# Convolution sums of three SSM groups in PSUM, and end-weighted x made from the turned x in PSUM

## The chip, the cores and the metric

The kernel runs on one core of a Trainium2 chip. The metric is the device time of one execution in microseconds; a comparison takes the median of several runs. The engines are TensorE (PE in the profile; PEld are its weight loads), VectorE (DVE), ScalarE (ACT), GpSimd (POOL) and the DMA queues, most of them issued by SyncE (SP). Everything is 4-byte floating point; matrix products of the projections run on pairs of rounded parts (`hi` and `lo`, type fp32r).

## The reference

One step of a decoder with two layers, for a prompt of 16 + 512 tokens and for 8 sequences of 4 new tokens (32 columns, "decode"). The first layer is sliding-window attention, the second a Mamba-2 mixer. The change touches the second layer. There, cut to what matters:

```
z, xbc, dt = split(u @ w_in)
conv    = sum over 4 taps of conv_w[tap] * xbc shifted by tap       # per channel
xs, B, C = split(silu(conv + conv_b))                                # the convolution's output
dt      = softplus(dt + dt_bias);  a = cumulative sum of dt * A in a chunk of 128
y_diag  = (C B^T * exp(a_i - a_j), causal) @ (xs * dt)
states  = B^T @ (xs * dt * exp(a_end - a))                           # the end-weighted x
state   = state * exp(a_end) + states
y       = y_diag + (C @ state) * exp(a) + d_skip * xs
out     = rmsnorm(y * silu(z)) @ w_out
```

The decode sequences do the same from given convolution rows and given states, which are returned renewed.

## The kernel before

Activations lie with channels on the 128 partitions and the 560 tokens in columns. Weights come in slabs of 1 MB: SyncE loads one, ScalarE rounds it (`w_hi_buf`, L702), GpSimd subtracts to get the low part (`w_lo_buf`, L621, four pieces of 128x512 a slab), and TensorE makes three products per depth step (L1211 to L1213). A projection is done in halves of about 272 to 280 columns into the two banks of `pp` in turn; TensorE starts a half when the half before last has been evacuated by VectorE (`p_evac`).

The mixer runs in four groups g = 0 to 3 ("first" to "fourth group"). A group has six tiles of convolution input: B and C (tiles 0, 1) and x (2 to 5). `conv_in` (L1886) evacuates a half from `pp` into `rb`; `conv_tap` (L1905) copies the decode sequences' old rows, saves the new ones in `cn`, makes the first tap as `tensor_scalar` (L1921) and the other three as `scalar_tensor_tensor` (L1923), each reading `rb` and the sum `cv` and writing `cv`. The four depend on each other; `link` makes each wait for the one before. Both buffers `cv0` and `cv1` lie in SBUF and are used in turn; `silu_conv` (L945) on ScalarE turns them into `bc` and `xc`.

In groups 1 to 3 VectorE's order is written out by hand (L2093 to L2127): taps of tiles 0 to 2 between the evacuations of the group's own x tiles and the norm of the previous group's y (`norm_y`, L2065, and `low_y`, L2073), taps of tiles 3 to 5 between the evacuations of the previous group's out projection (`add_out`, L1709).

Then the chunks follow, in units u = 0 to 5 of the order decode, 16 meta tokens, and four chunks of 128. TensorE's `part_a` (L1447) makes C B^T and turns B and x into `pS`, with tokens on the partitions; VectorE's `prepare` (L1970) makes from it `cbm`, `btok`, `xdt` = x times dt, and `xw` = `xdt` times the end weights `wend`. `mix` (L2005) multiplies the decay matrix `seg` by `cbm`. `seg` is loaded by DMA, then `a_j` is subtracted by GpSimd (L673), then clamped and exponentiated by ScalarE (L1057, L1059). TensorE's `part_b` (L1516) makes the y product from `xdt` and `seg` into `pT_` (L1530), the product with the state (L1540) and the new state from `btok` and `xw` (L1544) into `pO`. GpSimd decays the state (L634) and VectorE adds (L2026).

For the decode unit, `prepare` splits `xw` into the parts `x_parts`, from which TensorE makes the outer products (L1501) that renew the states (L2168). Its end weights times dt are made as `dtw` (32x8) each time.

PSUM tensors are `pp`, `pS`, `pT_` and `pO`, two banks of 512 columns each. `pT_` and `pO` are in use during the chunks and idle in the groups' convolution phases, up to the turning of `cn` (L1626) into `pT_`.

Of the kernel before, what the change touches and what calls it, by code (L numbers as in the profile page):

```python
# [24 lines left out]
ACT = mybir.ActivationFunctionType  # L25
# [35 lines left out]
LOW_FROM = 5  # L61
STACK = 3 * SAMPLE

C_ID, C_MASK, C_CAUS, C_SMASK, C_LAST, C_BTOK, C_BEND, C_SUM4, C_RESET, C_SATT = np.cumsum(
# [99 lines left out]
def build(nc, x_prompt, x_sample, cache_k, cache_v, state_conv, state_ssm, meta_tokens, norm_w,  # L164
# [53 lines left out]
    with ctx:  # L218
# [3 lines left out]
        def at(name, shape, dt=F32, offset=None):  # L222
            size = int(np.prod(shape[1:])) * 4
            size += -size % 32
            if offset is None:
                offset, top[0] = top[0], top[0] + size
            assert offset + size <= nc.sbuf_usable_end, (name, offset + size)
            where[name] = offset
            return nc.alloc_sbuf_tensor_at(name, shape, dt, offset=offset)
# [82 lines left out]
        ealast = at("ealast", [P, 5, 32])  # L312
        dtw = at("dtw", [SAMPLE, SSM_H])
        dec_s = at("dec_s", [P, 16, DEC_B])
# [23 lines left out]
        fS, fT, fO = flat(pS), flat(pT_), flat(pO)  # L338
        misc = pO[:, 1, :]

        def sem(name):
# [59 lines left out]
        def conv_tile(g, i):  # L401

            return [16 + g, 20 + g][i] if i < 2 else 4 * g + i - 2
# [30 lines left out]
        def part_of(g, part):  # L434

            edge = EARLY if g + 1 < GROUPS else COL[3]
            return slice(edge, T) if part else slice(N_META, edge)

        def scale_of(g):
# [242 lines left out]
        def _(act):  # L682
# [262 lines left out]
            def silu_conv(g, i):  # L945
                k = 6 * g + i
                if i == 2 and g:
# [3 lines left out]
                b = conv_bc(conv_tile(g, i))  # L951
                act.activation(dst[:, 0:PROMPT], cv[k % 2][:, 0:PROMPT], ACT.Silu, bias=b)
                act.activation(dst[:, PROMPT:T].rearrange("p (b s) -> p b s", b=DEC_B),
                               cv[k % 2][:, PROMPT + HALO:CONV_IN].rearrange("p (b s) -> p b s", s=SEG)[:, :, 0:DEC_S],
                               ACT.Silu, bias=b).then_inc(act_ready, 1)
# [207 lines left out]
        def _(pe):  # L1163
# [398 lines left out]
            for g in range(GROUPS):  # L1562
# [58 lines left out]
                if g:  # L1621
                    pe.wait_ge(d_done, 5 * g)
                else:
                    pe.wait_ge(pt_ready, UNITS * GROUPS)
# [53 lines left out]
        def _(dve):  # L1678
# [226 lines left out]
            def conv_tap(g, i, tap):  # L1905
                k = 6 * g + i
                r, w, ct = rb[i % 3], cv[k % 2], conv_tile(g, i)
                if tap == 0:
# [61 lines left out]
            def prepare(g, u):  # L1970
# [7 lines left out]
                mask = cst[0:32, C_SMASK:C_SMASK + 32] if c == 5 else cst[0:n, C_CAUS:C_CAUS + n]  # L1978
                if v == 0:
                    dve.wait_ge(dec_ready, 1)  # L1980
                if c == 5:

# [3 lines left out]
                                      ALU.subtract).then_inc(b_ready, 1)  # L1986
                    link(dve.tensor_tensor(dtw[:, :], tok2[0:n, 0, c, hs], wend[0:n, c, hs], ALU.mult))
                    link(dve.tensor_tensor(heads(xw[0:n, b, :], n), heads(pS[0:n, 1, :], n), per_head(dtw[:, :], n),
                                           ALU.mult))
                    dve.tensor_copy(x_parts[64:96, :], xw[0:n, b, :])  # L1990
# [6 lines left out]
                if c:  # L1997
                    dve.tensor_tensor(cbm[0:n, b, 0:n], pS[0:n, 0, 0:n], mask, ALU.mult)
                dve.tensor_copy(btok[0:n, b, :], pS[0:n, 0, P:2 * P])
                link(dve.tensor_tensor(heads(xdt[0:n, b, :], n), heads(pS[0:n, 1, :], n),  # L2000
                                       per_head(tok2[0:n, 0, c, hs], n), ALU.mult))
                dve.tensor_tensor(heads(xw[0:n, b, :], n), heads(xdt[0:n, b, :], n),
                                  per_head(wend[0:n, c, hs], n), ALU.mult).then_inc(xw_done, 1)
# [232 lines left out]
```

## Time and profile before

| | us |
|---|---|
| median of 3 runs | 1008.78 (1008.69 to 1009.45) |
| span of the profiled execution | 1008.4 |
| TensorE busy | 974.3 (97%) |
| VectorE busy | 580.3 (58%) |
| ScalarE busy | 469.5 (47%) |
| GpSimd busy | 363.7 (36%) |

The span is the profiled execution's own time from the first to the last instruction of the program; what lies around it isn't in the profile. TensorE's matmuls overlap, and their ends are modelled, so its busy share says how seldom it waits, not how near its peak it is. A timeline row has the start in us, the duration in us of all instructions merged in the row, engine, line, operation, what is written and read, shape and count; in brackets stands the engine's idle time before it and what ended it. "issue" as a releaser means that the engine waited for nothing that the profile can name. Rows by line have the shortest, the median and the longest duration in ns.

### The profile page before, as it was taken

What the parts mean: (1) busy time and instruction counts of PE and PEld (TensorE: products, weight loads), DVE (VectorE), ACT (ScalarE), POOL (GpSimd) and SP (SyncE); (2) the same over time, 40 slices, a digit from 0 to 9 for tenths busy, and PEclk for the clock granted to TensorE, in tenths of its full rate; (3) what the DMA queues carried; (4) which work ended last, traced back from release to release, by engine and by line L of the source; (5) the groups of instructions that cost most, each with busy time, mean ns of one, the idle gap of its engine ahead of it and who ended that gap; (6) DMA issues with size and microseconds to landing.
All of it is one profiled execution on the core that took longest, in us unless ns stands there. A gap on an engine that the chain in (4) does not pass through costs nothing.

```text
span 1008.4 us, 18539 instructions
## 1 busy us (share of the span) xinstructions
PE 974.3 (97%) x7372; PEld 896.8 (89%) x7372; DVE 580.3 (58%) x1433; ACT 469.5 (47%) x819; POOL 363.7 (36%) x275
## 2 busy tenths in 40 slices
PE   9999999999999999999998999999999999999988
PEld 8998999889998999879988789997899888997877
DVE  4225431444224421356687779957798577886872
ACT  6435713463235612467355455244552545526453
POOL 2331234134231143116442445425344253543600
PEclk9999999999999999999999999999999999999989
DMA  6522223322223222102425624256341662426203
GB/s 201 194 67 83 65 85 112 103 83 84 84 70 144 84 84 90 44 21 61 131 88 151 188 71 124 73 159 180 87 137 45 170 178 77 137 64 211 76 11 100
DMA packets 144117, 106.35 MB, mean 105 GB/s; under 512 B 10258, under 2 KB 135364, under 8 KB 143840
## 3 DMA queue, kind: packets, MB, share of 16 engines
q1 hardware_dynamic: 117208, 92.25, 29.5%
q10 hardware_dynamic: 26824, 12.93, 4.8%
q8 instruction: 58, 0.95, 0.4%
q14 instruction: 27, 0.22, 0.1%
HBM read 92.44 MB, written 16.79 MB: 108 GB/s over the span
## 4 chain that ended last, share of the span: by engine, by line
PE 83%; DVE 10%; issue 3%; ACT 1%; POOL 1%; DMA 0%; ACTq 0%; SPq 0%; DVEq 0%; POOLq 0%
PE pp L1211 20%; PE pp L1213 19%; PE pp L1212 19%; PE pS L1327 3%; PE pS L1551 2%; DVE cv L1923 2%; PE pT_ L1530 1%; PE pO L1540 1%; PE pO L1544 1%; PE pO L1373 1%; PE pO L1372 1%; PE pO L1491 1%; POOL w_lo_raw L621 1%; PE pS L1463 1%; DVE z L2065 1%
## 5 line engine op out<-in xcount | busy, mean ns | idle before, releaser
L621 POOL TENSOR_TENSOR w_lo_buf<-w_raw_buf,w_hi_buf 128x512 fp32r<-128x512 f32 x214 | 287.4, 1374 | 485.4 <-ACT w_hi_buf L702 247.6
L1211 PE MATMUL pp<-h_hi,w_hi_buf 128*128 128x280 f32 (+1 forms) x1248 | 378.1, 303 | 5.2 <-DVE rb L1897 2.8
L1213 PE MATMUL pp<-h_hi,w_lo_buf 128*128 128x280 f32 (+1 forms) x1248 | 362.9, 291 | 0.0
L1212 PE MATMUL pp<-h_lo,w_hi_buf 128*128 128x280 f32 (+1 forms) x1248 | 362.2, 290 | 0.0
L1211 PEld LDWEIGHTS pp<-h_hi,w_hi_buf 128*128 128x128 f32 x1248 | 235.2, 188 | 16.0 <-issue 8.0
L1212 PEld LDWEIGHTS pp<-h_lo,w_hi_buf 128*128 128x128 f32 x1248 | 235.2, 188 | 4.6 <-issue 4.1
L1213 PEld LDWEIGHTS pp<-h_hi,w_lo_buf 128*128 128x128 f32 x1248 | 235.2, 188 | 0.0
L702 ACT ACTIVATE w_hi_buf<-w_raw_buf 128x2048 fp32r<-128x2048 f32 (+1 forms) x55 | 104.0, 1892 | 23.4 <-DMA w_raw_buf<-in_w_ssm_in 16.4
L1709 DVE TENSOR_TENSOR x<-x,pp 128x272 f32<-128x272 f32 (+3 forms) x128 | 56.4, 440 | 79.5 <-PE pp L1213 78.7
L1211 PE MATMUL pp<-og_hi,w_hi_buf 128*128 128x280 f32 (+2 forms) x256 | 75.5, 295 | 1.7 <-DVE og_lo L1830 1.1
L1213 PE MATMUL pp<-og_hi,w_lo_buf 128*128 128x280 f32 (+2 forms) x256 | 74.5, 291 | 0.0
L1212 PE MATMUL pp<-og_lo,w_hi_buf 128*128 128x280 f32 (+2 forms) x256 | 74.4, 290 | 0.0
L1923 DVE SCALAR_TENSOR_TENSOR cv<-rb,par,cv 128x584 f32<-128x584 f32 x69 | 70.0, 1015 | 1.1
L1211 PE MATMUL pp<-y_hi,w_hi_buf 128*128 128x272 f32 (+2 forms) x224 | 66.7, 298 | 1.1 <-DVE x L1709 0.9
L1212 PE MATMUL pp<-y_lo,w_hi_buf 128*128 128x272 f32 (+2 forms) x224 | 64.5, 288 | 0.0
L1703 DVE TENSOR_TENSOR q<-pp,rs 128x280 f32<-128x280 f32 x32 | 14.4, 450 | 77.9 <-PE pp L1213 77.9
L1057 ACT ACTIVATE seg<-seg 128x1024 f32<-128x1024 f32 (+1 forms) x20 | 18.6, 932 | 83.1 <-issue 47.9
L1213 PE MATMUL pp<-y_hi,w_lo_buf 128*128 128x272 f32 x192 | 55.5, 289 | 0.0
L1211 PEld LDWEIGHTS pp<-og_hi,w_hi_buf 128*128 128x128 f32 x256 | 48.1, 188 | 2.7 <-issue 2.6
L1782 DVE TENSOR_TENSOR gate<-pp,rs 128x280 f32<-128x280 f32 x32 | 14.4, 450 | 62.8 <-PE pp L1213 62.8
L1212 PEld LDWEIGHTS pp<-og_lo,w_hi_buf 128*128 128x128 f32 x256 | 48.2, 188 | 0.2 <-issue 0.2
L1213 PEld LDWEIGHTS pp<-og_hi,w_lo_buf 128*128 128x128 f32 x256 | 48.1, 188 | 0.0
(338 smaller groups left out, 1724.1 us busy)
## 6 DMA issues: line engine op xcount, KB each, us to landing
w_raw_buf<-in_w_attn_in SPq DMA_DIRECT2D x16, 1024.0 KB, 5.2
w_raw_buf<-in_w_ssm_in SPq DMA_DIRECT2D x16, 1024.0 KB, 5.4
w_raw_buf<-in_w_attn_out SPq DMA_DIRECT2D x8, 1024.0 KB, 5.0
s_in<-in_state_ssm SPq DMA_DIRECT2D x32, 256.0 KB, 4.2
out<-s_in SPq DMA_DIRECT2D x32, 256.0 KB, 3.2
seg<-a_scratch ACTq DMA_DIRECT2D x16, 512.0 KB, 4.5
w_raw_buf<-in_w_ssm_out SPq DMA_DIRECT2D x8, 1024.0 KB, 5.6
w_raw_buf<-in_w_attn_in SPq DMA_DIRECT2D x8, 512.0 KB, 6.3
```

The lines of the kernel that those rows point to most:

```text
L621: ins = pool.tensor_tensor(low_buf(n)[:, piece], raw[n % RAW_SLOTS][:, piece], high_buf(n)[:, piece].bitcast(F32), ALU.subtract)
L702: act.activation(high_buf(n)[:, 0:m], raw[n % RAW_SLOTS][:, 0:m], ACT.Copy).then_inc(w_hi, 1)
L1057: act.activation(e, e, ACT.Relu, scale=-1.0).then_inc(clamped, 1)
L1211: pe.matmul(dst, hi[:, k, cols], a_hi[:, k, tk], start=(k == 0), stop=False)
L1212: pe.matmul(dst, hi[:, k, cols], a_lo[:, k, tk], start=False, stop=False)
L1213: mm = pe.matmul(dst, lo[:, k, cols], a_hi[:, k, tk], start=False, stop=(k == depth - 1))
L1327: mm = pe.matmul(fS[0:n, h * 256:h * 256 + nk], q[:, h, COL[c]:COL[c] + n], kq[:, k0:k0 + nk], start=True, stop=True)
L1551: mm = pe.matmul(pS[:, part, 0:tk.stop - tk.start], ones[:, :], xc[:, t, tk], start=(t == 0), stop=(t == HEADS - 1))
L1703: dve.tensor_tensor(dst[:, tk], bank(kind, s, tile, half), rs[:, tk], ALU.mult).then_inc(p_evac, 1)
L1709: dve.tensor_tensor(x[:, tile, tk], x[:, tile, tk], bank("out", s, tile, half), ALU.add).then_inc(p_evac, 1)
L1782: dve.tensor_tensor(gate[:, t, tk], bank("gate", s, t, half), rs[:, tk], ALU.mult).then_inc(p_evac, 1)
L1923: ins = dve.scalar_tensor_tensor(w[:, 0:CONV_OUT], r[:, tap:tap + CONV_OUT], conv_wc(tap, ct), w[:, 0:CONV_OUT], ALU.mult, ALU.add)
```

## The change

Four things are changed.

1. In groups 1 to 3 (k = 6g + i of 6 or more) the sums of the taps are kept in PSUM: `taps_of(k)` gives 587 columns at the end of `pT_` for even tiles and of `pO` for odd ones, in the place of `cv0` and `cv1`. All four taps write there, three read there, and ScalarE's activation reads there. Group 0 stays in SBUF.
2. TensorE's turning of `cn` into `pT_` waits in groups 1 to 3 for the activation of tile 4 too, which reads `pT_`.
3. `wend` is multiplied by `tok2` (dt) once for all groups, in three instructions ahead of group 0's decode unit; `dtw` is gone.
4. `xw` is made from the turned x in `pS` and the multiplied `wend`, no longer from `xdt`; nothing waits for `xdt` between.

```diff
@@ -60,6 +60,7 @@
+TAPS_AT = 1024 - CONV_IN
@@ -310,7 +311,6 @@
-        dtw = at("dtw", [SAMPLE, SSM_H])
@@ -337,6 +337,7 @@
+        cv_psum = [fT[:, TAPS_AT:1024], fO[:, TAPS_AT:1024]]
@@ -436,6 +437,10 @@
+        def taps_of(k):
+
+            return cv[k % 2] if k < 6 else cv_psum[k % 2]
+
@@ -949,9 +954,9 @@
-                act.activation(dst[:, 0:PROMPT], cv[k % 2][:, 0:PROMPT], ACT.Silu, bias=b)
+                act.activation(dst[:, 0:PROMPT], taps_of(k)[:, 0:PROMPT], ACT.Silu, bias=b)
...
@@ -1620,6 +1625,7 @@
                 if g:
                     pe.wait_ge(d_done, 5 * g)
+                    pe.wait_ge(act_ready, 6 * g + 5)
@@ -1904,7 +1910,7 @@
             def conv_tap(g, i, tap):
                 k = 6 * g + i
-                r, w, ct = rb[i % 3], cv[k % 2], conv_tile(g, i)
+                r, w, ct = rb[i % 3], taps_of(k), conv_tile(g, i)
@@ -1977,16 +1983,19 @@
                 if v == 0:
+
                     dve.wait_ge(dec_ready, 1)
+                    for m, c0, c1 in ((P, 1, 5), (16, 0, 1), (SAMPLE, 5, 6)):
+                        ins = dve.tensor_tensor(wend[0:m, c0:c1, :], wend[0:m, c0:c1, :], tok2[0:m, 0, c0:c1, :], ALU.mult)
+                    link(ins)
...
-                    link(dve.tensor_tensor(dtw[:, :], tok2[0:n, 0, c, hs], wend[0:n, c, hs], ALU.mult))
-                    link(dve.tensor_tensor(heads(xw[0:n, b, :], n), heads(pS[0:n, 1, :], n), per_head(dtw[:, :], n),
-                                           ALU.mult))
+                    link(dve.tensor_tensor(heads(xw[0:n, b, :], n), heads(pS[0:n, 1, :], n),
+                                           per_head(wend[0:n, c, hs], n), ALU.mult))
@@ -1997,9 +2006,9 @@
-                link(dve.tensor_tensor(heads(xdt[0:n, b, :], n), heads(pS[0:n, 1, :], n),
-                                       per_head(tok2[0:n, 0, c, hs], n), ALU.mult))
-                dve.tensor_tensor(heads(xw[0:n, b, :], n), heads(xdt[0:n, b, :], n),
+                dve.tensor_tensor(heads(xdt[0:n, b, :], n), heads(pS[0:n, 1, :], n),
+                                  per_head(tok2[0:n, 0, c, hs], n), ALU.mult)
+                dve.tensor_tensor(heads(xw[0:n, b, :], n), heads(pS[0:n, 1, :], n),
                                   per_head(wend[0:n, c, hs], n), ALU.mult).then_inc(xw_done, 1)
```

VectorE in group 1's convolution phase, before; `rb_115` is the input of tile 2, `cv_117` and `cv_116` the sums of tiles 1 and 2:

```order
643 L1923 SCALAR_TENSOR_TENSOR cv_117<-rb_114,par,cv_117 128x584 x2
644 L1897 TENSOR_TENSOR rb_114<-pp,rs 128x280
645 L1913 COPY rb_115<-pS 128x8x3
646 L1919 COPY cn<-rb_115 128x3
647 L1920 COPY cn<-rb_115 128x24
648 L1921 TENSOR_SCALAR cv_116<-rb_115,par 128x584
649 L1923 SCALAR_TENSOR_TENSOR cv_116<-rb_115,par,cv_116 128x584
```

And in the changed kernel:

```order
645 L1929 SCALAR_TENSOR_TENSOR pO<-rb_114,par,pO 128x584 x2
646 L1903 TENSOR_TENSOR rb_114<-pp,rs 128x280
647 L1919 COPY rb_115<-pS 128x8x3
648 L1925 COPY cn<-rb_115 128x3
649 L1926 COPY cn<-rb_115 128x24
650 L1927 TENSOR_SCALAR pT_<-rb_115,par 128x584
651 L1929 SCALAR_TENSOR_TENSOR pT_<-rb_115,par,pT_ 128x584
```

No instruction has another place; only where the sum lies is different.

VectorE ahead of group 0's decode unit, before (from the first z evacuation to the first part of x):

```order
537 L2152 TENSOR_TENSOR z<-pp,rs 128x272
538 L1983 CAST b_parts<-pS 32x128
539 L1984 CAST b_parts<-pS 32x128
540 L1985 TENSOR_TENSOR b_parts<-pS,b_parts 32x128
541 L1987 TENSOR_TENSOR dtw<-tok_146,wend 32x8
542 L1988 TENSOR_TENSOR xw<-pS,dtw 32x512
543 L1990 CAST x_parts<-xw 32x512
```

And in the changed kernel:

```order
537 L2161 TENSOR_TENSOR z<-pp,rs 128x272
538 L1989 TENSOR_TENSOR wend<-wend,tok_146 128x128
539 L1989 TENSOR_TENSOR wend<-wend,tok_146 16x32
540 L1989 TENSOR_TENSOR wend<-wend,tok_146 32x32
541 L1993 CAST b_parts<-pS 32x128
542 L1994 CAST b_parts<-pS 32x128
543 L1995 TENSOR_TENSOR b_parts<-pS,b_parts 32x128
544 L1997 TENSOR_TENSOR xw<-pS,wend 32x512
545 L1999 CAST x_parts<-xw 32x512
```

Three multiplies stand ahead of everything of this unit, once in the program, and `dtw` is missing here and in the other three groups.

## Rows read from the trace of the kernel before

**Rows 1.** The page: the span, and part 1 (busy time, share, instructions).
```profile
span 1008.4 us, 18539 instructions
...
PE 974.3 (97%) x7372; PEld 896.8 (89%) x7372; DVE 580.3 (58%) x1433; ACT 469.5 (47%) x819; POOL 363.7 (36%) x275
```

**Rows 2.** Waits of TensorE from 560 us: total us, times, longest us.
```profile
PE pT_ L1530 <- issue: 8.2, 12, 1.0
PE pS L1551 <- ACT xc L1124: 4.0, 1, 4.0
PE pp L1211 <- DVE rb L1901: 2.3, 3, 1.2
PE pS L1501 <- DVE xdt L1994: 1.5, 3, 0.5
...
PE pp L1211 <- DVE x L1709: 1.3, 3, 0.4
PE pp L1211 <- DVE rb L1897: 0.8, 2, 0.5
```

**Rows 3.** Timeline of VectorE, second group (start, us, line, out<-in, count).
```profile
705.53 1.40 DVE L2002 TENSOR_TENSOR xw<-xdt,wend 128x512 f32<-128x512 f32 x1
...
708.03 1.74 DVE L2012 TENSOR_TENSOR seg<-seg,cbm 128x1024 f32<-128x1024 f32 x1 [0.49 <-ACT seg L1059]
```

**Rows 4.** Timeline of GpSimd, the same stretch.
```profile
695.88 2.29 POOL L673 TENSOR_TENSOR seg<-seg,tok 128x1024 f32<-128x1024 f32 x1 [5.14 <-DMA seg<-a_scratch]
...
699.14 1.89 POOL L673 TENSOR_TENSOR seg<-seg,tok 128x1024 f32<-128x1024 f32 x1
705.34 1.04 POOL L634 TENSOR_TENSOR state<-state,ealast 128x512 f32<-128x512 f32 x1 [4.31 <-PE pO L1544]
706.34 2.35 POOL L673 TENSOR_TENSOR seg<-seg,tok 128x1024 f32<-128x1024 f32 x1
```

**Rows 5.** Timeline of ScalarE, the same stretch.
```profile
706.93 1.06 ACT L1059 ACTIVATE seg<-seg 128x1024 f32<-128x1024 f32 x1
```

**Rows 6.** VectorE by line: count, duration ns min/median/max, first and last start.
```profile
L2002 DVE TENSOR_TENSOR xw<-xdt,wend x20: 691/1247/1631, 561.1 to 961.0; 128x512 f32<-128x512 f32 x16, 16x512 f32<-16x512 f32 x4
...
L2000 DVE TENSOR_TENSOR xdt<-pS,tok x20: 668/681/682, 560.4 to 960.3; 128x512 f32<-128x512 f32 x16, 16x512 f32<-16x512 f32 x4
...
L2168 DVE SCALAR_TENSOR_TENSOR s_in<-s_in,dec_s,pS x128: 328/344/349, 542.7 to 930.0; 128x128 f32<-128x128 f32 x128
...
L1923 DVE SCALAR_TENSOR_TENSOR cv<-rb,par,cv x69: 817/827/1747, 496.9 to 903.3; 128x584 f32<-128x584 f32 x69
...
L1921 DVE TENSOR_SCALAR cv<-rb,par x23: 508/518/1564, 496.3 to 900.0; 128x584 f32<-128x584 f32 x23
...
L1987 DVE TENSOR_TENSOR dtw<-tok,wend x4: 269/282/960, 537.7 to 911.3; 32x8 f32<-32x8 f32 x4
```

**Rows 7.** Timeline of VectorE, convolution phases of the second and third groups.
```profile
620.94 2.60 DVE L1923 SCALAR_TENSOR_TENSOR cv<-rb,par,cv 128x584 f32<-128x584 f32 x2
...
624.71 1.56 DVE L1921 TENSOR_SCALAR cv<-rb,par 128x584 f32<-128x584 f32 x1
626.31 1.75 DVE L1923 SCALAR_TENSOR_TENSOR cv<-rb,par,cv 128x584 f32<-128x584 f32 x1
...
743.53 2.33 DVE L2065 SCALAR_TENSOR_TENSOR z<-z,par,rg 128x160 f32<-128x160 f32 x4
```

**Rows 8.** Timeline of GpSimd, second group's convolution phase.
```profile
621.15 6.28 POOL L621 TENSOR_TENSOR w_lo_buf<-w_raw_buf,w_hi_buf 128x512 fp32r<-128x512 f32 x4 [5.36 <-ACT w_hi_buf L702]
```

**Rows 9.** Groups by line and shape of VectorE: count, busy us, mean ns.
```profile
L2023 DVE COPY state<-pO 128x512 f32<-128x512 f32 x4 | 2.7, 684 | 0.0
```

**Rows 10.** Timeline of VectorE, end of the second group's out projection.
```profile
655.97 0.44 DVE L1709 TENSOR_TENSOR x<-x,pp 128x272 f32<-128x272 f32 x1 [0.22 <-PE pp L1213]
657.48 0.44 DVE L1709 TENSOR_TENSOR x<-x,pp 128x272 f32<-128x272 f32 x1 [1.07 <-PE pp L1213]
```

**Rows 11.** Timeline of ScalarE, activation of tile 4, second group.
```profile
650.47 0.74 ACT L952 ACTIVATE xc<-cv,par 128x528 f32<-128x528 f32 x1 [3.63 <-DVE cv L1923]
```

More of the change, by code:

```diff
@@ L951, in silu_conv @@
                 b = conv_bc(conv_tile(g, i))
-                act.activation(dst[:, 0:PROMPT], cv[k % 2][:, 0:PROMPT], ACT.Silu, bias=b)
+                act.activation(dst[:, 0:PROMPT], taps_of(k)[:, 0:PROMPT], ACT.Silu, bias=b)
                 act.activation(dst[:, PROMPT:T].rearrange("p (b s) -> p b s", b=DEC_B),
-                               cv[k % 2][:, PROMPT + HALO:CONV_IN].rearrange("p (b s) -> p b s", s=SEG)[:, :, 0:DEC_S],
+                               taps_of(k)[:, PROMPT + HALO:CONV_IN].rearrange("p (b s) -> p b s", s=SEG)[:, :, 0:DEC_S],
                                ACT.Silu, bias=b).then_inc(act_ready, 1)
```

## The prediction

> **What bounds the kernel now.** I read the page first: the span is 1008.4 us and TensorE is busy for 974.3 of it [rows 1]. So nothing that VectorE saves is worth anything unless TensorE waits for it. The profiled execution's span stands 0.4 us below the median of the runs (1008.78), which I take as what lies around the span; the sum is made against 1008.4 and 0.4 is added at the end.
>
> Next the waits of TensorE, from 560 us on, where the groups' chunks begin [rows 2]. The reader is to see four kinds. Twelve waits before the product with `seg` (L1530), 8.2 us, put down to "issue", since what was waited for is a semaphore chain and not a neighbour; five before a projection for the evacuation into `rb` (L1901 2.3 us in three, L1897 0.8 in two), in the convolution phases; three of 0.5 us before the decode products (L1501); and one of 4.0 us in the last group. That is the purse: about 13 us can be touched by this change at all, the 4.0 us only by moving as a whole.
>
> Then what stands behind each kind. For L1530 I read the same stretch on three engines [rows 3 to 5]. VectorE makes `xw` at 705.53 from two SBUF tensors and is busy 1.40 us with it. GpSimd decays the state from 705.34 to 706.38 and then subtracts in `seg` from 706.34 for 2.35 us. The same subtraction took 1.89 us at 699.14, when no such VectorE instruction lay beside it. The rows are those of two engines that exclude each other: `xw` stands still until the decay ends, then holds the subtraction up for 2.35 - 1.89 = 0.46 us; ScalarE's exponent is ready at 707.99, but the multiply in `seg` (708.03, 1.74 us) ends at 709.77, which is 1.08 us after the subtraction's end at 708.69. TensorE waits for that multiply. The minimum, median and maximum by line say who is open to this [rows 6]: `xw<-xdt,wend` 691/1247/1631 ns, the taps 817/827/1747 and 508/518/1564, but `xdt<-pS,tok`, the same size with one source in PSUM, 668/681/682 in all 20, and the state update with a PSUM source 328/344/349 in all 128.
>
> **The chunks: xw from the turned x in PSUM.** 20 instructions go, 20 of the form of `xdt<-pS,tok` come: 0.68 each, never stretched. VectorE saves up to 0.72 us in a stretched one, but it idles before the multiply anyway; only what GpSimd gains reaches TensorE. At the third unit's chunk, `xw` holds the subtraction of 695.88 up by 2.29 - 1.89 = 0.40; at the next one by 0.46. After that, ScalarE's 707.99 against GpSimd's 708.23 says what is late next: it leaves the full 0.46 standing, with 0.24 to spare. At the last chunk no subtraction follows, so nothing is gained. A group gains 0.86; in each of the four groups the pattern has two such subtractions, so 3.4 us, of which I take 3.3. Bounds: 0 if ScalarE's chain or the landing of `seg` takes over at once, 4 groups by 3 waits by the mean wait of 0.68, that is 8.2, if all of them vanish. The dependence between `xdt` and `xw` goes too; not counted.
>
> A rule speaks against this edit. The Trainium skill, VectorE: DVE Perf Modes, section on the TRN2 errata, gives a VectorE instruction out of PSUM 62 cycles more fixed cost than one out of SBUF, 0.065 us each at its clock. The row disagrees: with the PSUM source 681, with both in SBUF 691 at best [rows 6]. By the rule `xw` would still be shorter than its median, and the sum would lose at most some 0.3 us where it lies on the path.
>
> **The decode unit.** `dtw` goes: 0.28 in three groups [rows 6], directly on the path from the turned x to the decode products, where TensorE waits 0.5 each time [rows 2]. So 0.8 us. In the first group `dtw` took 0.96 (the maximum), and three multiplies of `wend` by `tok2` come, once, ahead of everything of that unit. All have two SBUF sources, and a slab's split runs beside them. Priced as `dtw`: 3 x 0.27 = 0.8 to 3 x 0.96 = 2.9, less 0.96: from -0.1 to +1.9. I take +0.4, near the low end, since short instructions in a row mostly pass in one gap between GpSimd's.
>
> **The convolution: 18 tiles in groups 1 to 3.** Each has one tap of L1921 and three of L1923. Second and third groups show it [rows 7, 8]: from 620.94, beside GpSimd's split from 621.15, two taps take 2.60 instead of 2 x 0.82, a first tap 1.56 instead of 0.52, another tap 1.75. Three stretches of about 1 us stand ahead of the evacuation for which TensorE waited its 1.2 us. With the sum in PSUM a tap has one SBUF tensor source, as the 128 state updates have. No row shows VectorE writing PSUM, so a tap is bounded: 0.77 (the 0.82, less 0.05) below; above, if reading and writing one PSUM bank took turns, twice the slope per element. That slope is (827 - 344) / (584 - 128) = 1.06 ns, so 827 + 584 x 1.06 = 1.45 us. I take 0.82, the row of the same operation. The first tap: 0.52 at best as now. L2023, a one-source copy of 512 elements out of PSUM, takes 0.684 [rows 9], so 584 elements take 0.684 + 72 x 1.06 ns = 0.76. I take 0.76, +0.24 on a clean one.
>
> The Trainium skill, VectorE: DVE Perf Modes, section "Why PSUM operands drop a tier", says that any PSUM operand keeps a one-source instruction on 4-byte data from going two elements per cycle. It names operands in general; the trace shows it for a source only. By it the sum is the one I make; if a PSUM destination alone kept the fast mode, it would be 0.7 us lower.
>
> What reaches TensorE: the waits behind stretched taps, 1.2 in the second group, 0.3 in the third, 0.5 and 0.2 in the fourth, 2.2 of the 3.1 us [rows 2], go whole: in each of the three phases stretched taps stand ahead of the evacuation waited for (the longest is 1.75 [rows 6]), and 0.9 us of stretch outweighs 0.5 of wait. The one of 1.0 us in the third group does not: ahead of it stand four `norm_y` instructions with two SBUF tensors (743.53, 2.33 us) [rows 7], unchanged. The first taps before them are clean today, so +0.24 falls on it, and about as much on each sister evacuation in the second and fourth groups, which come just in time: +0.7. Net -1.5. The waits for `x<-x,pp` (1.3 us) [rows 2] come from `low_y`, two SBUF sources, unchanged.
>
> In the out projection, where twelve more taps stand between evacuations, a tile takes TensorE 1.51 us (655.97 to 657.48) [rows 10], and an evacuation with a tap at most 0.44 + 0.82 = 1.26: TensorE is waited for, not VectorE, and that stays. A first tap with its three small copies comes to some 1.7, once in four tiles; the second bank covers it.
>
> **The new wait.** TensorE's turning of `cn` now waits for the activation of tile 4. In the second group that begins at 650.47 [rows 11] and ends about a microsecond later, while TensorE is still delivering out tiles at 657.48 [rows 10] and has one z projection after. Cost 0, with some 6 us to spare. Behind it would stand all z projections. ScalarE now reads its input from PSUM; its 0.74 us changes by hundredths, in idle time.
>
> **Sum.** 1008.4 - 3.3 - 0.8 + 0.4 - 1.5 = 1003.2, with 0.4 around it 1003.6 us, 0.5% faster.
>
> **Rivals.**
> 1. ScalarE takes over in the chunks. Its exponent stands only 0.24 before the new end of GpSimd's subtraction, and behind it lies a loop (evacuation, three adds, DMA issue, two activations) that GpSimd's gain doesn't shorten. If that loop, not GpSimd, sets the pace, the 3.3 go: 1008.4 - 0.8 + 0.4 - 1.5 + 0.4 = 1006.9. For it: the closeness. Against it: the multiply ended 1.08 after GpSimd, not after ScalarE.
> 2. The convolution's gain is given back: freed taps bring VectorE earlier to `norm_y` and `low_y`, which meet GpSimd's split instead. In the second group the `norm_y` of this kind is clean and could become the third group's, +1.0. Then the convolution's net is 0: 1008.4 - 3.3 - 0.8 + 0.4 + 0.4 = 1005.1.
> 3. Slower. Taps that read and write the same PSUM bank take 1.45 us. It decides from 1.51 - 0.44 = 1.07 us per tap: above that, a tap and an evacuation no longer fit into an out tile. Nine such taps in the out phase cost 1.45 - 1.07 = 0.38 each, 3.4; nine ahead of it 0.6 each, 5.6, less the 3.1 that stretching costs today: about 6 a group, 18 in all, against 3.7 saved elsewhere: 1008.4 - 3.7 + 18 + 0.4 = 1023. Nothing in the trace has that form; for it only that no row excludes it.
> 4. The change frees VectorE and GpSimd, and neither term reaches TensorE, which is at 97% [rows 1]: rivals 1 and 2 together, 1008.4 - 0.8 + 0.4 + 0.4 = 1008.4. For it: most of what VectorE saves is saved while it idles.
>
> **How the numbers follow.** A change under 0.2% (2 us) can't be told from none here. Forecast case 0.60; rival 1 0.14; rival 2 0.12; rival 3 0.05; rival 4 0.09. Under 1006.76: the forecast case, rival 2 and half of rival 1: 0.79. Within 0.2%: the other half and most of rival 4: 0.14. Slower: rival 3 and the tail of 4: 0.07. The range must leave out no more than 0.2. Downwards, more of the 8.2 us at L1530 may go than I counted: 1000.8. Upwards, up to rival 1: 1007.3.
>
> **What would show it.** `xw` at 0.68 in all 20; the 128x1024 subtractions of `seg` at 1.89 with none above 2.0 except behind the multiply; L1530's waits down from 8.2 to about 5. Taps of 584 elements in groups 1 to 3 with a maximum near their median, about 0.82; first taps at 0.76. The 1.2 us wait of the second group gone, the 1.0 of the third still there. Wrong would be: taps above 1.07; L1530's waits as they were, with ScalarE's exponent as the last to arrive; a new wait of TensorE at the turning of `cn`.

## The result and the profile after

The changed kernel takes 1000.07 us (median of 4, 997.68 to 1002.94) against 1008.79 us beside it: a ratio of 0.9914, 95% interval 0.9892 to 0.9935. In a second session it took 1001.11 us (1000.03 to 1002.61), ratio 0.9918 [0.9902, 0.9934]. So it is 8 to 9 us faster, where 5.2 had been forecast; 1000.07 lies 0.7 us below the forecast range. The changed kernel's single times lie some 5 us apart, by how long TensorE ran at half clock; its profiled execution is one of the longer ones (1002.94). Two lines of the page answer to [rows 1]:

```profile
span 1000.9 us, 18538 instructions
...
PE 973.2 (97%) x7372; PEld 898.3 (90%) x7372; DVE 555.2 (55%) x1432; ACT 468.5 (47%) x819; POOL 347.7 (35%) x275
```

VectorE's busy time fell by 25 us and GpSimd's by 16; TensorE's stayed. What moved are the waits. The view of TensorE's waits from 560 us on (total us, times, longest), to be held against [rows 2]:

```profile
PE pT_ L1535 <- issue: 4.6, 8, 1.1
PE pS L1556 <- ACT xc L1129: 4.1, 1, 4.1
PE pS L1465 <- DVE s_in L2177: 2.1, 4, 1.4
...
PE pS L1506 <- DVE xdt L2003: 0.5, 3, 0.2
PE pp L1216 <- DVE x L1715: 0.4, 1, 0.4
```

The five waits for the evacuation into `rb` are gone, 0.9 of the 1.3 us for `x` too, and the wait for the product with `seg` went from 8.2 to 4.6 us. The 2.1 us before L1465 hold one wait of 1.4 in the fourth group.

The view by line (count, ns min/median/max, first and last start) says that none of these is stretched any more, against [rows 6]: `xw`, the subtraction in `seg`, and in groups 1 to 3 the taps with their sum in PSUM. (The three new multiplies in the first group are; they come below.)

```profile
L2011 DVE TENSOR_TENSOR xw<-pS,wend x20: 669/681/682, 563.4 to 953.6; 128x512 f32<-128x512 f32 x16, 16x512 f32<-16x512 f32 x4
...
L678 POOL TENSOR_TENSOR seg<-seg,tok x20: 607/1898/1903, 531.0 to 947.3; 128x1024 f32<-128x1024 f32 x16, 32x256 f32<-32x256 f32 x4
...
L1929 DVE SCALAR_TENSOR_TENSOR pT_<-rb,par,pT_ x27: 821/825/832, 610.3 to 889.3; 128x584 f32<-128x584 f32 x27
...
L1927 DVE TENSOR_SCALAR pT_<-rb,par x9: 816/822/826, 609.1 to 885.1; 128x584 f32<-128x584 f32 x9
```

Where the time went is read best from the starts of TensorE's work. I took in each trace the first start of four kinds of instruction: the turning of the old convolution rows (a group's start), the first out projection, the turning of `cn`, the first decode product (L1501, L1506). The lengths between them, as difference to the kernel before, in us (before's own lengths from its one trace):

| phase | before | changed kernel | forecast |
|---|---|---|---|
| first group, to the turning of `cn` | 41.2 | -0.5 | 0 |
| first group, to the first decode product | 7.3 | +1.90 | +0.4 |
| second to fourth group, the same | 6.04, 6.04, 6.03 | -0.32, -0.32, -0.31 | -0.28 each |
| chunks, first to third group | 61.3, 61.3, 61.4 | -0.80, -1.15, -0.88 | -0.86 each |
| convolution up to the out projection, second to fourth group | 28.42, 28.62, 28.31 | -1.60, -1.80, -1.49 | -1.5 in all |
| out projection and first z half, the same | 28.44, 28.15, 28.45 | -0.76, -0.48, -0.77 | 0 |

The changed kernel's three convolution phases have one length, 26.82 us, and no wait stands in them. The first phase, which the change doesn't touch, is 0.2 to 0.7 us shorter than in before's profile in all runs that don't touch it; I leave it out of the account. Between two executions of the changed kernel the other lengths agree within 0.03 us, the chunks within 0.3 where the clock is the same.

The fourth group's chunks have to be read with the clock. The rows are stretches of the trace: length, busy us of PE, PEld, DVE, ACT and POOL with counts, then the granted clock. Before:

```profile
914.70:972.10 57.40, 50.06 (x374) 41.56 (x374) 43.98 (x90) 27.52 (x41) 21.93 (x15) 0.91 0.43 128
```

The changed kernel in its profiled execution, and in another one (run `e8_same_again`):

```profile
906.50:964.50 58.00, 51.14 (x374) 42.68 (x374) 39.67 (x90) 27.64 (x42) 20.56 (x15) 0.88 0.43 127
```

```profile
908.00:961.50 53.50, 47.75 (x374) 39.43 (x374) 39.34 (x89) 27.57 (x42) 21.57 (x15) 0.97 0.47 137
```

A mean of 0.91 is 10.3 us at the lower level of 1.2 GHz (0.09 x 57.4 x 2), 0.88 is 13.9 us, 0.97 is 3.2 us. Between the two executions of the same kernel, 10.7 us more of it cost 4.5, so 0.42 us each, an estimate from one pair. Before's 7.1 us more than in the last row are worth 3.0 of its 3.9 us: the chunks gained about 0.9 here too. So without the clock the change is worth some 9.7 us, by this estimate: -6.9 in the convolution, -3.7 in the chunks, -0.95 in three decode units, +1.9 in the first.

### The profile page after: what moved, and what is told of

The parts are those of the page before. It is cut to its first block, busy times and chain, and to the rows that moved or that the text cites. A ratio compares the mean times of both kernels' runs of the same rounds, so it can differ in the third digit from the quotient of the medians.

```text
span 1000.9 us, 18538 instructions
## 1 busy us (share of the span) xinstructions
PE 973.2 (97%) x7372; PEld 898.3 (90%) x7372; DVE 555.2 (55%) x1432; ACT 468.5 (47%) x819; POOL 347.7 (35%) x275
## 4 chain that ended last, share of the span: by engine, by line
PE 87%; DVE 8%; issue 3%; ACT 1%; DMA 1%; ACTq 0%; POOL 0%; SPq 0%; DVEq 0%; POOLq 0%
PE pp L1216 21%; PE pp L1218 21%; PE pp L1217 20%; PE pS L1332 3%; PE pS L1556 2%; PE pT_ L1535 1%; PE pO L1549 1%; PE pO L1545 1%; PE pO L1378 1%; PE pO L1377 1%; DVE s_in L2177 1%; PE pO L1496 1%; PE pS L1468 1%; PE pS L1326 1%; PE pp L1268 1%
## 5 line engine op out<-in xcount | busy, mean ns | idle before, releaser
L626 POOL TENSOR_TENSOR w_lo_buf<-w_raw_buf,w_hi_buf 128x512 fp32r<-128x512 f32 x214 | 274.8, 1316 | 490.5 <-ACT w_hi_buf L707 251.2
L807 ACT ACTIVATE sm<-sm,nm,crow 128x256 f32<-128x256 f32 (+2 forms) x80 | 42.3, 530 | 8.2 <-DVE ds L1754 8.2
```

The costliest lines, as they stand in the source:

```text
L626: ins = pool.tensor_tensor(low_buf(n)[:, piece], raw[n % RAW_SLOTS][:, piece], high_buf(n)[:, piece].bitcast(F32), ALU.subtract)
L807: act.activation(p, p, ACT.Exp, bias=nm[0:n, v % 2, h:h + 1], scale=crow[0:n, cc + h:cc + h + 1], accum_out=den[0:n, v % 2, h:h + 1])
```

## The experiments

All are made from the changed kernel; "before" is the kernel before. Phases are compared as above, always with before's one trace; medians with those of before on the same chip. The phases come from one profiled execution of each kernel.

**One part alone.** `e1_taps_only` has the sums in PSUM, the rest as before:

```diff
...
-                    for m, c0, c1 in ((P, 1, 5), (16, 0, 1), (SAMPLE, 5, 6)):
...
+                    link(dve.tensor_tensor(dtw[:, :], tok2[0:n, 0, c, hs], wend[0:n, c, hs], ALU.mult))
...
-                dve.tensor_tensor(heads(xw[0:n, b, :], n), heads(pS[0:n, 1, :], n),
+                dve.tensor_tensor(heads(xw[0:n, b, :], n), heads(xdt[0:n, b, :], n),
...
```

> Only the sums of the taps of groups 1 to 3 lie in PSUM; xw is made from xdt and dtw stays, as before the change. Theory A (the convolution is worth more than the idle rows of TensorE showed, because waits below the modelled end of a matmul, the norm's wait and late starts of out tiles count too): each of the three convolution and out-projection phases is 2.3 us shorter than before, 6.9 in all, the chunks and decode units unchanged, so a median of about 1002; GpSimd's subtraction in seg is at 2.3 us again where xw lies beside it. Theory B (the 6.9 us need the freed chunks too, since they shift VectorE against GpSimd's splits): the phases give back no more than the 1.5 us in all that were forecast, so about 1007.

Measured: 1001.59 us, ratio 0.9923 [0.9894, 0.9953]. The three convolution and out phases are 2.35, 2.28 and 2.28 us shorter than before, 6.91 in all; chunks and decode units are within 0.02 of before. The subtraction in `seg` is stretched again, up to 2.87 us:

```profile
L679 POOL TENSOR_TENSOR seg<-seg,tok x20: 607/1898/2872, 531.9 to 946.9; 128x1024 f32<-128x1024 f32 x16, 32x256 f32<-32x256 f32 x4
```

`e2_xw_only` has the other part:

```diff
             def taps_of(k):
-            return cv[k % 2] if k < 6 else cv_psum[k % 2]
+            return cv[k % 2]
```

> Only xw from the turned x with multiplied end weights, dtw gone; all sums of the taps stay in SBUF. Theory A (parts add up): the chunks gain 0.8 to 1.1 us a group, the decode units of groups 1 to 3 0.32 each, and the first group's decode unit loses 1.8, so a median 1.9 us below before, about 1007; the convolution phases are as before within 0.3 each. Theory B (what was seen in the convolution came from the shifted chunks): the convolution phases are 1 us or more shorter each, so 1004 or less.

Measured: 1006.78 us, ratio 0.9981 [0.9966, 0.9997]. Chunks of the second and third groups -0.91 and -0.86 (the first's have a half-clock stretch here), decode units -0.32 three times and +1.89 in the first group, convolution and out phases within 0.26 of before. Theory A both times: the convolution's 6.9 us need nothing from the chunks, and the parts add up, but for 0.25 us in the fourth group, which `e2_xw_only` has too and which is lost in the 1.49 of the taps: the phase is at its 26.82 us without it.

**Which taps.** `e3_early_tiles` and `e4_late_tiles` keep in PSUM the sums of tiles 0 to 2 and of tiles 3 to 5 alone:

```diff
-            return cv[k % 2] if k < 6 else cv_psum[k % 2]
+            return cv_psum[k % 2] if k >= 6 and k % 6 < 3 else cv[k % 2]      # e3; e4: >= 3
```

> As the changed kernel, but in groups 1 to 3 only the sums of tiles 0 to 2 lie in PSUM, those of tiles 3 to 5 (made between the evacuations of the out projection) in SBUF. Theory A (late starts in the out projection, hidden in no idle row, are worth 0.5 us a group): the part up to the last evacuation into rb gains 1.8 a group as in the changed kernel, the out-projection part gains nothing, so it is 0.5 x 3 = 1.5 us longer than the changed kernel. Theory B, the prediction's (TensorE never waits for taps in the out projection): within 0.3 of the changed kernel in every phase.

> The other half: in groups 1 to 3 only the sums of tiles 3 to 5 lie in PSUM, those of tiles 0 to 2 in SBUF. Theory A: the waits of TensorE behind stretched taps (1.2 us in the second group) and behind norm_y (1.0 us in the third) are back, 1.8 a group, 5.4 in all over the changed kernel; the out-projection part keeps its 0.5 a group. Theory B, the prediction's (norm_y's wait has nothing to do with the taps and its loss was an accident of the shift): only some 2.2 us come back in all, and norm_y's rows in the third group stay at 1.3 us, not 2.3.

Measured: 1001.00 us, 0.9914 [0.9881, 0.9947], and 1005.87 us, 0.9971 [0.9955, 0.9987]. By phase, in the three groups, less than before (0.24 of e4's stands in `e2_xw_only` as well, without any tap in PSUM):

| | up to the out projection | out projection and first z half |
|---|---|---|
| e3, early tiles | 1.60, 1.80, 1.49 | 0.32, 0.00, 0.29 |
| e4, late tiles | -0.04, 0.01, 0.24 | 0.46, 0.48, 0.46 |
| both (changed kernel) | 1.60, 1.80, 1.49 | 0.76, 0.48, 0.77 |

The two add up again. Out of the 6.9 us, 4.9 are the early taps' before the out projection, 1.4 the late taps' in it, 0.6 the early taps' through `low_y`. e3's out parts are 1.4 us longer than the changed kernel's, as theory A had it; its median doesn't show that beside the clock's spread.

And `norm_y` in the third group, whose 1.0 us wait I had said would stay. VectorE's timeline has its four instructions, before at 743.53 with 2.33 us [rows 7]; here with the late tiles alone:

```profile
743.31 2.36 DVE L2074 SCALAR_TENSOR_TENSOR z<-z,par,rg 128x160 f32<-128x160 f32 x4
```

with the early tiles alone:

```profile
742.84 1.27 DVE L2074 SCALAR_TENSOR_TENSOR z<-z,par,rg 128x160 f32<-128x160 f32 x4
```

and GpSimd's timeline of the late-tiles run:

```profile
733.42 6.36 POOL L626 TENSOR_TENSOR w_lo_buf<-w_raw_buf,w_hi_buf 128x512 fp32r<-128x512 f32 x4 [5.49 <-ACT w_hi_buf L707]
744.21 6.13 POOL L626 TENSOR_TENSOR w_lo_buf<-w_raw_buf,w_hi_buf 128x512 fp32r<-128x512 f32 x4 [4.43 <-ACT w_hi_buf L707]
```

With the taps in SBUF the split of 733 runs for 6.36 us and the next begins at 744.21, under `norm_y`. With the early tiles alone in PSUM `norm_y` is over at 744.11, and the next split begins at 744.53. In the changed kernel the two splits take 5.35 and 5.08, and `norm_y` is over (740.65 + 1.27 = 741.92) before the second begins:

```profile
731.46 5.35 POOL L626 TENSOR_TENSOR w_lo_buf<-w_raw_buf,w_hi_buf 128x512 fp32r<-128x512 f32 x4 [5.49 <-ACT w_hi_buf L707]
742.30 5.08 POOL L626 TENSOR_TENSOR w_lo_buf<-w_raw_buf,w_hi_buf 128x512 fp32r<-128x512 f32 x4 [5.49 <-ACT w_hi_buf L707]
```

```profile
740.65 1.27 DVE L2074 SCALAR_TENSOR_TENSOR z<-z,par,rg 128x160 f32<-128x160 f32 x4
```

The waits of the late-tiles run show the old ones back:

```profile
PE pp L1216 <- DVE rb L1903: 1.5, 3, 0.9
...
PE pp L1216 <- DVE rb L1907: 1.2, 2, 1.0
```

So `norm_y` was stretched because stretched taps ahead of it had made VectorE late.

**Reading or writing.** `e7_in_turn` sends the sum to and fro, so that each place occurs as a source and as a destination:

```diff
...
+                src, w = (cv[k % 2], w) if tap == 2 else (w, cv[k % 2])
                 ins = dve.scalar_tensor_tensor(w[:, 0:CONV_OUT], r[:, tap:tap + CONV_OUT], conv_wc(tap, ct),
-                                               w[:, 0:CONV_OUT], ALU.mult, ALU.add)
+                                               src[:, 0:CONV_OUT], ALU.mult, ALU.add)
...
```

> As the changed kernel, but the sums of groups 1 to 3 go to and fro: the first tap writes PSUM, the second reads PSUM and writes SBUF, the third reads SBUF twice and writes PSUM, the fourth reads PSUM and writes SBUF. Theory A (what keeps a tap from standing still beside GpSimd is that it reads only one SBUF tensor; where it writes plays no part): the second and fourth taps have a maximum of about 0.83 us, the third is stretched up to 1.75 where a split lies beside it. Theory B (the place written counts as well): the second and fourth, which write SBUF, are stretched too, or the third is not. Time: between the changed kernel and the one with all sums in SBUF, 1 to 3 us over the changed one.

Measured: 1000.77 us (one run). Its convolution and out phases are 0.7 us longer than the changed kernel's in all, less than the 1 to 3 us expected. By line:

```profile
L1930 DVE SCALAR_TENSOR_TENSOR cv<-rb,par,pT_ x18: 809/816/824, 610.7 to 891.3; 128x584 f32<-128x584 f32 x18
L1930 DVE SCALAR_TENSOR_TENSOR cv<-rb,par,pO x18: 814/816/823, 620.3 to 897.1; 128x584 f32<-128x584 f32 x18
L1930 DVE SCALAR_TENSOR_TENSOR cv<-rb,par,cv x15: 825/827/1720, 496.7 to 524.4; 128x584 f32<-128x584 f32 x15
L1930 DVE SCALAR_TENSOR_TENSOR pT_<-rb,par,cv x9: 822/1367/1819, 611.6 to 889.6; 128x584 f32<-128x584 f32 x9
L1930 DVE SCALAR_TENSOR_TENSOR pO<-rb,par,cv x9: 825/828/1681, 622.8 to 895.8; 128x584 f32<-128x584 f32 x9
```

All 36 taps that read PSUM and write SBUF lie between 809 and 824 ns. Of those that read SBUF twice the longest has 1.82 us, though it writes PSUM. Theory A: the place read decides, the place written does not. The Trainium skill, SBUF — State Buffer, section "Who interferes with whom", says so as a rule: a VectorE instruction with at most one SBUF input, outside its two-port modes, doesn't contend with GpSimd. These rows agree.

**The first group's multiplies.** In the changed kernel VectorE and GpSimd stand so there (the three take 0.76, 1.27 and 1.32 us, each ending within 0.15 us of the end of one of GpSimd's pieces):

```profile
537.30 3.20 DVE L1989 TENSOR_TENSOR wend<-wend,tok 128x128 f32<-128x128 f32 x3 [1.62 <-PE pS L1468]
```

```profile
535.41 5.06 POOL L626 TENSOR_TENSOR w_lo_buf<-w_raw_buf,w_hi_buf 128x512 fp32r<-128x512 f32 x4 [3.63 <-DVE cv L1950]
```

and TensorE waits behind them, where it was 1.5 us before:

```profile
PE pS L1506 <- DVE xdt L2003: 3.4, 1, 3.4
```

`e5_late_mult` leaves only the 32 decode rows' multiply in place:

```diff
-                    for m, c0, c1 in ((P, 1, 5), (16, 0, 1), (SAMPLE, 5, 6)):
-                        ins = dve.tensor_tensor(wend[0:m, c0:c1, :], wend[0:m, c0:c1, :], tok2[0:m, 0, c0:c1, :], ALU.mult)
-                    link(ins)
...
+                    if g == 0:
+                        link(dve.tensor_tensor(wend[0:n, c, :], wend[0:n, c, :], tok2[0:n, 0, c, :], ALU.mult))
...
+                    if g == 0 and pair == 1:
+                        dve.tensor_tensor(wend[:, 1:5, :], wend[:, 1:5, :], tok2[:, 0, 1:5, :], ALU.mult)
+                        link(dve.tensor_tensor(wend[0:16, 0, :], wend[0:16, 0, :], tok2[0:16, 0, 0, :], ALU.mult))
```

> As the changed kernel, but of the three multiplies of wend by tok2 only that of the 32 decode rows stays in the first group's decode unit (at dtw's old place, behind the parts of B); the other two stand behind the z evacuation of the second pair of states, where VectorE idled 1.8 us. Theory A (the three cost 1.9 us because each waited for a piece of GpSimd's split, with TensorE waiting behind): TensorE's wait before the first decode product goes from 3.4 back to about 1.5 us, the two moved ones (0.3 us, at most 2.1 beside a split) cost TensorE nothing, so 1.8 us less than the changed kernel; and the half-clock stretch that followed the 3.4 us wait in three of four profiles with it does not come there, which is up to 3.5 us more in those. Theory B (VectorE's idle time there is taken up by the split too): the third pair of states starts late and the gain is under 1 us.

Measured: 997.89 us, ratio 0.9880 [0.9862, 0.9899]. The wait is 1.5 again, the phase 1.90 us shorter than in the changed kernel, and the two moved multiplies take what they cost alone, with VectorE idle behind them:

```profile
PE pS L1506 <- DVE xdt L2002: 1.5, 1, 1.5
```

```profile
550.08 0.28 DVE L2182 TENSOR_TENSOR wend<-wend,tok 128x128 f32<-128x128 f32 x1
550.28 0.17 DVE L2183 TENSOR_TENSOR wend<-wend,tok 16x32 f32<-16x32 f32 x1
552.05 2.15 DVE L2176 SCALAR_TENSOR_TENSOR s_in<-s_in,dec_s,pS 128x128 f32<-128x128 f32 x8 [1.60 <-PE pS L1506]
```

The clock: the same stretch, 538 to 552 us, in `e2_xw_only` (with the 3.4 us wait) and here (without):

```profile
538.00:552.00 14.00, 10.59 (x68) 10.36 (x67) 9.38 (x24) 7.10 (x16) 2.00 (x2) 0.76 0.43 119
```

```profile
538.00:552.00 14.00, 12.48 (x102) 11.25 (x101) 9.17 (x28) 7.91 (x18) 1.26 (x2) 1.00 0.76 196
```

Seven profiles have that wait (the changed kernel's two, e2, e3, e4, e7, e10): in this stretch the first of the changed kernel has 1.00, the other six 0.76 or 0.88. The five profiles with 1.5 us (before, e1, e5, e6, e9) all have 1.00. One half-clock stretch cost the second execution of the changed kernel 1.4 us in the chunks behind it. In those six the chunks of the first group are 0.9 to 2.5 us longer than in the changed kernel's first profile. So the multiplies cost 1.9 us, and where the clock fell, 0.9 to 2.5 more were lost behind them. What preceded each of these falls was the longer wait of TensorE. That the wait brings the fall is argued from these twelve profiles, not shown: one profile has the wait without the fall.

`e8_same_again` is the changed kernel once more, beside e5 to e7.

> The changed kernel once more, on the same chip as the three beside it. Every theory: about 1000 us, single runs between 997.5 and 1003 by how many half-clock stretches of TensorE fall in them; in the profile the 3.4 us wait ahead of the first group's decode products is there, and behind it a half-clock stretch in some executions and not in others.

Measured: 1001.11 us (1000.03 to 1002.61), ratio 0.9918 [0.9902, 0.9934], with the wait and the half-clock stretch. e5's interval lies wholly below this one's.

**One evacuation earlier.** `e6_late_mult_early_evac` adds to e5:

```diff
-                    conv_taps(g, 3)
+                    for tap in range(3):
+                        conv_tap(g, 3, tap)
+                    conv_in(g, 4, 0)
+                    conv_tap(g, 3, 3)
...
-                    conv(g, 4)
+                    conv_in(g, 4, 1)
+                    conv_taps(g, 4)
```

> As the kernel before this one, and in the first group's convolution phase the evacuation of the first half of tile 4 stands ahead of the last tap of tile 3, instead of behind that tap and the four multiplies for ea_in and dec_in. Theory A (TensorE's 1.6 us wait there is for this evacuation alone): that wait goes, 1.6 us less, nothing else moves. Theory B (behind it the second half's evacuation or dec_in is late next): 0.8 us or less. If A holds on both, this is the fastest, about 3.4 us below the changed kernel.

Measured: 996.68 us, ratio 0.9875 [0.9856, 0.9894]; the phase is 0.43 us shorter than e5's, not 1.6. Theory B in substance, but what is late next is GpSimd: the wait of 1.6 went, and one of 1.5 came, which ends at 529.99. It stands before the first product with a new slab, and the view of waits puts it down to the slab's low part:

```profile
PE pp L1216 <- POOL w_lo_buf L626: 1.5, 1, 1.5
```

GpSimd's timeline has that split ending at 529.89, and VectorE's has the taps of tile 4 beside it, three of them 4.44 us long, and the evacuation behind them, over at 528.19, 1.8 us before TensorE went on:

```profile
523.78 6.11 POOL L626 TENSOR_TENSOR w_lo_buf<-w_raw_buf,w_hi_buf 128x512 fp32r<-128x512 f32 x4 [14.33 <-ACT w_hi_buf L707]
```

```profile
523.01 4.44 DVE L1929 SCALAR_TENSOR_TENSOR cv<-rb,par,cv 128x584 f32<-128x584 f32 x3
...
527.76 0.43 DVE L1903 TENSOR_TENSOR rb<-pp,rs 128x280 f32<-128x280 f32 x1
```

The expectation of the next run took the evacuation for what was late.

`e9_tile4_psum` puts that tile's sum into PSUM as well:

```diff
-            return cv[k % 2] if k < 6 else cv_psum[k % 2]
+            return cv[k % 2] if k < 6 and k != 4 else cv_psum[k % 2]
...
```

> As e6, and in the first group the sums of tile 4 lie in PSUM too (TensorE's turning of cn then waits for that tile's activation there as well). In e6 the three later taps of that tile took 4.44 us beside a split of GpSimd, and TensorE then waited 1.5 us at 528 for the evacuation behind them. Theory A (a tap with its sum in PSUM doesn't stand still there either): the three take 2.5 us, the evacuation comes 1.6 us earlier (0.3 of the 1.9 goes to the slower first tap), TensorE's wait goes whole, and the convolution phase of the first group is 1.5 us shorter than in e6. Theory B (the three multiplies between the taps and the evacuation wait for TensorE's own sums, whose end is then what is late): the wait shrinks by less than 1 us. The half-clock stretches are as before in either case, so a median about 995.5 by A.

Measured: 996.17 us, ratio 0.9859 [0.9839, 0.9879]. The taps do what A says:

```profile
525.96 2.57 DVE L1931 SCALAR_TENSOR_TENSOR pT_<-rb,par,pT_ 128x584 f32<-128x584 f32 x3
```

but the phase is only 0.43 us shorter than e6's, where theory A had 1.5. Neither theory named the engine. The split beside these taps takes 5.09 us now (from 526.37 to 531.46) instead of 6.11, and TensorE's wait of 0.4 before the new slab ends at 531.56, again 0.1 us behind the split; the evacuation was over at 529.26. Counted from the group's start the split began 0.59 us later than in e6 and so ended 0.44 earlier, which is what the phase gained. Ahead of it TensorE waits 0.6 us for an evacuation at 515, which it doesn't in e6's execution; that this made the split begin later is likely, but not shown.

The chunks behind are 1.2 us longer than e5's. There GpSimd waited for `seg` to land, first here, then in e5:

```profile
573.67 1.90 POOL L678 TENSOR_TENSOR seg<-seg,tok 128x1024 f32<-128x1024 f32 x1 [6.57 <-DMA seg<-a_scratch]
```

```profile
570.86 1.90 POOL L678 TENSOR_TENSOR seg<-seg,tok 128x1024 f32<-128x1024 f32 x1 [5.37 <-DMA seg<-a_scratch]
```

The longest landing took 6.3 us in this execution, 5.2 in e5. GpSimd's wait differs by 1.20, as the chunks do. Whether the later landing is chance or comes of the change wasn't tried. The intervals of e5, e6 and e9 overlap, so their times don't rank them; each lies below that of `e8_same_again`, and they are the fastest seen, 1.2 to 1.4% below before.

**The dependence between xdt and xw.** `e10_link_kept`:

```diff
-                dve.tensor_tensor(heads(xdt[0:n, b, :], n), heads(pS[0:n, 1, :], n),
+                link(dve.tensor_tensor(heads(xdt[0:n, b, :], n), heads(pS[0:n, 1, :], n),
```

> As the changed kernel, but xw still waits for xdt in the chunks, although it no longer reads it. Theory A (the gain in the chunks is what GpSimd no longer waits for xw): the chunk phases of the second and third groups are within 0.1 us of the changed kernel's, since VectorE has time before the multiply in seg. Theory B (the dependence that went is part of the gain): about 0.05 to 0.1 us in each of five units comes back, 0.3 to 0.5 us a group.

Measured: 1003.19 us (one run; 13.9 us at half clock in the fourth group's chunks, as in the changed kernel's own profile). The second and third groups' chunks are 0.15 and 0.06 us shorter than in `e8_same_again`, so nothing comes back: theory A, the dependence was no part of the chunks' gain.

## Why the prediction was partly wrong

The step that failed is the convolution term: forecast -1.5 us, measured -6.9. The other terms together were forecast at -3.7 and measured at some -2.8, so the time fell below the range by this one step.

1. **The chunks** (-3.3): right. Measured -0.80, -1.15, -0.88 and about -0.9. `xw` is 0.68 in all 20; the subtraction has a maximum of 1.90 against 2.35. At the place of [rows 3 to 5] the three engines now stand so:

```profile
703.70 0.68 DVE L2011 TENSOR_TENSOR xw<-pS,wend 128x512 f32<-128x512 f32 x1
...
706.30 1.29 DVE L2021 TENSOR_TENSOR seg<-seg,cbm 128x1024 f32<-128x1024 f32 x1 [0.85 <-ACT seg L1064]
```

```profile
704.62 1.90 POOL L678 TENSOR_TENSOR seg<-seg,tok 128x1024 f32<-128x1024 f32 x1
```

```profile
705.21 1.06 ACT L1064 ACTIVATE seg<-seg 128x1024 f32<-128x1024 f32 x1
```

GpSimd ends at 706.52, ScalarE at 706.27, the multiply (starting at 706.30) at 707.59: 1.07 behind GpSimd, as the 1.08 before. Alone this multiply takes 1.23 (the median by line), so it would have ended at 707.53 had only ScalarE counted: GpSimd is still what is late here, by 0.06 us, where the forecast had 0.24 to spare. Rivals 1 and 4, which give the chunks nothing, are refuted by the phases.

2. **The decode unit** (-0.8): right, -0.95 in the three groups.

3. **The first group's multiplies** (+0.4): mis-sized, it was +1.9, the upper end of the bounds given. The failed argument was that short instructions pass in one gap between GpSimd's. They don't: the three took 3.20 us beside four pieces of about 1.27 (5.06 us), about one piece each. The row of one such instruction, `dtw` with 0.96, was the right price and I took it for the exception. The clock's part was not foreseen at all.

4. **The convolution** (-1.5): this is the step that failed; it measured -6.9. The 5.4 us between them are four errors of reading:
   - *Waits priced by their idle rows* (1.7 us). TensorE's waits ahead of the out projection show 3.2 us (the 2.2 of the forecast and `norm_y`'s 1.0), and 4.9 us of phase went with them. The 1.2 in the second group stood for 1.60. In the trace it is a product that starts 1.44 us after the one before it, where 0.13 is usual; the idle row counts from the modelled end of that one, and some further late starts of 0.1 us each have no row at all.
   - *`norm_y`'s wait kept* (1.0 us, in the same 4.9). "Unchanged" was true of the instruction, not of its place beside the split, which the early taps had moved (e3, e4).
   - *First taps charged* (0.7 us). They did get slower, 0.82 instead of 0.52 (forecast 0.76), but ahead of the out projection TensorE waits for nothing any more. In the out projection one half starts 0.08 us late behind such a tap.
   - *The out projection put at 0* (2.0 us). "An evacuation with a tap at most 1.26" used the clean tap. Beside a split it was not clean. Before, in the second group:

```profile
644.94 0.44 DVE L1709 TENSOR_TENSOR x<-x,pp 128x272 f32<-128x272 f32 x1 [0.34 <-PE pp L1213]
645.29 1.60 DVE L1923 SCALAR_TENSOR_TENSOR cv<-rb,par,cv 128x584 f32<-128x584 f32 x1
646.93 0.44 DVE L1709 TENSOR_TENSOR x<-x,pp 128x272 f32<-128x272 f32 x1
647.28 1.38 DVE L1923 SCALAR_TENSOR_TENSOR cv<-rb,par,cv 128x584 f32<-128x584 f32 x1
648.70 0.44 DVE L1709 TENSOR_TENSOR x<-x,pp 128x272 f32<-128x272 f32 x1
```

The evacuations lie 1.99 and 1.77 us apart (644.94, 646.93, 648.70) where a half takes TensorE 1.51 [rows 10]. At first the second bank covers that. Then, in TensorE's timeline, the halves start at 649.21, 650.84, 652.65 and 654.26: 1.63, 1.81 and 1.61 us apart, 0.52 us lost in all. Each late start is short against the modelled end of the matmul before it, so no wait stands in the rows. In the changed kernel:

```profile
646.25 0.44 DVE L1715 TENSOR_TENSOR x<-x,pp 128x272 f32<-128x272 f32 x1 [0.33 <-PE pp L1218]
646.60 0.82 DVE L1929 SCALAR_TENSOR_TENSOR pT_<-rb,par,pT_ 128x584 f32<-128x584 f32 x1
647.76 0.44 DVE L1715 TENSOR_TENSOR x<-x,pp 128x272 f32<-128x272 f32 x1 [0.33 <-PE pp L1218]
```

1.51 us apart (646.25, 647.76), VectorE idles, and TensorE's halves start 1.51 apart throughout here. The 0.52 less the 0.08 of the first tap is about the 0.46 to 0.48 a group of e4. The other 0.3 in two groups are `low_y`, also called unchanged: its first two instructions in the out projection of the second group took 1.31 and 1.41 us before and take 1.00 and 1.40 now, and the half of TensorE behind them starts 0.32 us earlier.

5. **The rivals.** Rival 2 (gain given back) was turned round: freed taps took `norm_y` out of the split's way. Rival 3 (reading and writing one bank, 1.45 us a tap) is refuted: 821 to 832 ns for 27, 817 to 831 for 27. Its price was also mis-added, since the 3.1 us that stretching costs are those of all three groups and were taken off in each: by its own figures about 24 us, not 18. The new wait at the turning of `cn` cost nothing, as forecast.

6. **The sum.** The profiled execution of the changed kernel took 2.0 us more than its span (1002.94, 1000.9). The 0.4 "around the span" compared an execution's span with other executions' median. By the same 2.0 us, an estimate, before's profiled execution took about 1010.4 us, 1.6 over its median. Since the 0.4 stood in the sum on both sides, it moved nothing.

## What to carry to other kernels

Where an engine on the path runs in lockstep with another, price its spacing by the stretched instructions of that stretch, not by the median: a wait that is short against the modelled end of the instruction before it shows in no idle row, but in the distance of its starts. "This instruction is unchanged" says nothing of its duration when what stands before it moves. A few short instructions with two SBUF sources beside GpSimd's long ones cost here about one long one each, so they belong where both engines idle. And before an evacuation is moved forward, look at what else the same product waits for: in e6 it was the slab's low part.

## What the hardware showed beyond that

- A tap that reads and writes the same PSUM columns costs 0.82 us for 584 columns, as with all operands in SBUF (0.827) undisturbed. The first tap (`tensor_scalar`) loses its faster form by the destination alone: 0.822 against 0.517.
- ScalarE's activation of 528 columns takes 0.702 us out of PSUM and 0.735 out of SBUF.
- TensorE at the lower clock level cost about 0.42 us per us in the fourth group's chunks, an estimate from two executions, the granted clock being given to two digits. TensorE was busy for 47.75 of the 53.50 us there.
